# Value products of two attention heads, issued alternately into the two halves of the array's columns

## The reference

```python
def attend(q, k, v):
    s = jnp.einsum('bqhd,bkhd->bhqk', q, k).astype(jnp.float32) * MLA_SCALE
    p = jax.nn.softmax(s, axis=-1).astype(v.dtype)
    return jnp.einsum('bhqk,bkhd->bqhd', p, v)
```

## Time and profile before

| | |
|---|---|
| median of 3 runs | 2709.06 us (2708.07 to 2709.28) |
| profiled execution | 2707.86 us |
| span of its trace | 2706.1 us, 26605 instructions |
| PE busy | 2178.7 us (81%) |
| DVE busy | 1637.9 us (61%) |
| ACT busy | 1122.2 us (41%) |
| POOL busy | 816.2 us (30%) |
| DMA | 940.05 MB, mean 347 GB/s |
| L1664, the edited products | 320 MATMUL records, 46.5 us busy |

### The profile page before, as it was taken

The page is one execution under the profiler, slowest core; times in us unless marked ns, Lnnn a source line. Parts: engine busy times, 40 slices in busy tenths (PEclk is TensorE's granted clock), DMA queues, the critical chain, the costliest instruction groups (busy, mean ns, idle before and its releaser), DMA issues.

```text
span 2706.1 us, 26605 instructions
## 1 busy us (share of the span) xinstructions
PE 2178.7 (81%) x8372; PEld 1023.3 (38%) x8372; DVE 1637.9 (61%) x4029; ACT 1122.2 (41%) x3248; POOL 816.2 (30%) x772
## 2 busy tenths in 40 slices
PE   6998889877788677885777777697889987777776
PEld 4766655432344233441121111176674321221111
DVE  1134476678886756777667775333627666777654
ACT  3233354555773434545343333332423343333333
POOL 0000134434444334344434333100004443343331
PEclk8988999878899889998999999995899999999999
DMA  7883299999999999999999999720018999999997
GB/s 317 316 335 134 72 403 407 409 352 398 413 380 414 421 409 412 417 420 421 421 421 421 421 421 421 312 80 1 17 52 346 425 425 426 426 425 426 426 426 307
DMA packets 133660, 940.05 MB, mean 347 GB/s; under 512 B 14864, under 2 KB 16144, under 8 KB 23312
## 3 DMA queue, kind: packets, MB, share of 16 engines
q0 software_dynamic: 110592, 805.36, 71.9%
q1 hardware_dynamic: 22496, 130.31, 12.2%
q10 hardware_dynamic: 432, 2.70, 0.3%
HBM read 937.26 MB, written 1.05 MB: 347 GB/s over the span
## 4 chain that ended last, share of the span: by engine, by line
DMA 43%; PE 35%; DVE 10%; ACT 8%; issue 3%; POOL 1%; SPq 0%; DVEq 0%; POOLq 0%; ACTq 0%
DMA fast<-uv_dram,idx 26%; DMA mix<-uv_dram,idx 14%; PE bank L1757 11%; PE bank L1716 5%; PE bank L1487 4%; DVE fast L1358 3%; PE bank L1680 2%; DMA qring<-wq_dram 2%; PE bank L1572 2%; PE bank L1451 1%; PE bank L1481 1%; PE bank L1725 1%; ACT diag L933 1%; ACT coef L930 1%; PE bank L1459 1%
## 5 line engine op out<-in xcount | busy, mean ns | idle before, releaser
L1757 PE MATMUL bank<-fast,diag 128*64 128x512 f32 x1956 | 800.4, 657 | 244.3 <-ACT diag L933 242.7
L628 POOL DMA_INDIRECT fast<-uv_dram,idx x489 | 522.4, 1068 | 1422.2 <-PE bank L1757 686.1
L1358 DVE SCALAR_TENSOR_TENSOR fast<-fast,hrow 128x1024 f32<-128x1024 f32 x489 | 598.4, 1225 | 344.9 <-DMA fast<-uv_dram,idx 340.5
L929 ACT ACTIVATE gact<-araw 128x1 f32<-128x1 f32 x768 | 154.4, 201 | 903.5 <-DVE fast L1358 550.5
L1757 PE MATMUL bank<-mix,diag 128*64 128x512 f32 x816 | 382.8, 621 | 102.5 <-ACT diag L933 100.9
L1757 PEld LDWEIGHTS bank<-fast,diag 128*64 128x64 f32 x1956 | 190.7, 144 | 704.7 <-ACT diag L933 458.6
L1358 DVE SCALAR_TENSOR_TENSOR mix<-mix,hrow 128x1024 f32<-128x1024 f32 x204 | 250.3, 1227 | 180.4 <-DMA mix<-uv_dram,idx 175.8
L628 POOL DMA_INDIRECT mix<-uv_dram,idx x204 | 209.5, 1027 | 285.0 <-PE bank L1757 263.8
L933 ACT ACTIVATE diag<-con,coef 128x64 f32<-128x64 f32 x768 | 267.1, 348 | 25.2
L930 ACT ACTIVATE coef<-gact,wts 128x1 f32<-128x1 f32 x768 | 226.2, 295 | 24.9
L1757 PEld LDWEIGHTS bank<-mix,diag 128*64 128x64 f32 x816 | 92.6, 138 | 342.8 <-ACT diag L933 228.3
(11 more groups left out here) (231 smaller groups left out, 2616.6 us busy)
## 6 DMA issues: line engine op xcount, KB each, us to landing
fast<-w_dram SPq DMA_DIRECT2D x72, 1024.0 KB, 8.8
qring<-wq_dram SPq DMA_DIRECT2D x40, 576.0 KB, 8.2
back<-w_dram SPq DMA_DIRECT2D x20, 1024.0 KB, 9.4
fast<-uv_dram,idx POOLq DMA_INDIRECT x489, 17.4
mix<-wq_dram SPq DMA_DIRECT2D x8, 576.0 KB, 5.5
mix<-uv_dram,idx POOLq DMA_INDIRECT x204, 23.9
fast<-uq_dram SPq DMA_DIRECT2D x4, 576.0 KB, 3.5
xT<-x_dram ACTq DMA_DIRECT2D x1, 2048.0 KB, 9.0
```

Of the source, the lines that this page charges most:

```text
L628: g.indirect_dma_start(slot(e, m), None, uv_tabs[e], bass.IndirectOffsetOnAxis(idx[:, Q % 2, n:n + 1], 0)).then_inc(landed[place], 16)
L929: link(a.activation(gact[:, n:n + 1], araw[:, Q % 2, n:n + 1], ACT.Gelu))
L1358: v.scalar_tensor_tensor(out=u, in0=u, scalar=1.0, in1=hrow[:, (2 * i + half) % 3, :], op0=ALU.mult, op1=ALU.mult, accum_out=araw[:, Q % 2 ...
L1757: mm = t_.matmul(acc[half, f * 512:(f + 1) * 512], diag[:, j % DIAGS, :], slot(e, j)[:, D + f * 512:D + (f + 1) * 512], start=(j % SLOTS < ...
```

## The change

The products of the two heads of a pair are issued in one step at time 9, where head 0's were at 7 and head 1's at 9. Within it the loop over key chunks is outside and that over heads inside, so consecutive products go to different halves of the columns. The step waits for both heads' transposed shares; each head's last product still adds one to `pv_mm`. No other generator is edited.

```diff
                 for j in range(8):
-                    for f in range(2):
-                        i, h = 2 * j + f, 2 * (j % 4) + f
-                        yield ATT_AT + ATT_STEP * j + 7 + 2 * f
-                        if f == 0 and j:
-                            t_.wait_ge(attn_out.sem, attn_out.at(p, j))
-                        t_.wait_ge(pt_ready.sem, pt_ready.at(p, i + 1))
-                        n = chunks(p)
-                        for c in range(n):
-                            vv = vr if c < 2 else vc
+                    yield ATT_AT + ATT_STEP * j + 9
+                    if j:
+                        t_.wait_ge(attn_out.sem, attn_out.at(p, j))
+                    t_.wait_ge(pt_ready.sem, pt_ready.at(p, 2 * j + 2))
+                    n = chunks(p)
+                    for c in range(n):
+                        vv = vr if c < 2 else vc
+                        for f in range(2):
+                            h = 2 * (j % 4) + f
                             mm = t_.matmul(bank[3][64 * f:64 * f + 64, 0:P], vv[:, c % 2, h * VD:(h + 1) * VD], pt[:, f, c, :],
                                            start=(c == 0), stop=(c == n - 1))
-                        mm.then_inc(pv_mm.sem, 1)
+                            if c == n - 1:
+                                mm.then_inc(pv_mm.sem, 1)
```

## The result

The changed kernel takes 2718.49 us (median of 6 runs) against 2708.57 for the kernel before (6 runs): ratio 1.0038, 95% interval 1.0024 to 1.0051. It is slower by about 10 us. The time lies in the range (2706 to 2719), near its upper end, but the likeliest case, no measurable change, isn't what happened. It lies outside the forecast's own range of 2708 to 2716; only the part that was added for the rivals takes it in.

What follows compares the result with a forecast made beforehand. Chain of waits: 43% DMA, 35% TensorE, limits differing by stage. Stage 3 -0.04, stage 0 -0.15, stage 1 +3.0 make +2.8 us on 2707.86: 2710.7 (2711.9 beside the median); range 2708 to 2716, widened for rivals to 2706 to 2719.

Steps and rivals of the forecast that it cites:

- the likeliest case, no measurable change: Whole kernel: time within about 0.2% (5.4 us) of the unchanged kernel, chance 0.72.
- The overlap: Value products of both heads, alternating column halves: 1.02 us in place of 2.04, saving 1.02 us per pair at full clock.
- The new stall: TensorE waits before head 1's transpose for ScalarE's copy of head 0's: 0.76 us per pair in stage 3, 0.54 in stage 0.
- Pairs of 4.81 us: Stage 3 (layer 1's attention): a pair takes 4.81 us against 4.98, -0.17 us, five times.
- stage 3 level: Layer 1's attention: pairs -0.85, head -0.95 and tail +1.76 us, in all -0.04 us.
- Stage 0 level if the clock rises at the same time: Layer 0's context tokens: half-clock pairs gain, full-clock pairs about level, tail +1.11 us; in all -0.15 us.
- The clock rival for stage 0: Layer 0's context tokens: holes in each pair delay the full clock until after the last scores; +9 us, 2721 us, chance 0.14.
- Stage 1, +3.0 us: Layer 0's latent tokens, between expert gathers: later ScalarE copies add 3.0 us, first-order sum 3.8, bounds 0 and 7.6.
- the added wait: Stage 1: seven copies of head 0's transposed shares wait about 1.09 us more, delaying GELU, diagonals and exponentials; 3.8 us summed.
- TensorE's gain is hidden, because each pair's diagonals come late anyway: Stage 1: TensorE's saved time was counted as no gain, since its expert products wait for the diagonals.
- a moved clock: Sign of a wrong prediction: stage 0's clock was to rise near 234 us, as before; no size given.
- No overlap: All three stages: the heads' products run one after another, 2.04 us, and the stalls stay; +24 us, 2733 us, chance 0.06.

Runs made afterwards that it cites:

- run 6: Changed kernel with a second buffer for the copied shares and the heads' products one after the other, not alternating: 2702.61 us, 0.9979 of the kernel before.
- Run 4: Changed kernel with a second buffer for the copied transposed shares, used by pairs with odd j: 2694.87 us, 0.9952 of the kernel before.
- run 3: Kernel before with the new order in stages 0 and 3 only, stage 1 keeping the old order: 2709.52 us, 1.0010 of the kernel before.
- run 2: Kernel before with the new order in stage 1 only, stages 0 and 3 keeping the old order: 2714.70 us, 1.0024 of the kernel before.
- run 5: Kernel before; in stage 1 ScalarE's copy of head 0's transposed shares also waits for the previous pair's head 1 products: 2711.44 us, 1.0010.
- run 9: New order in stage 1 only, with head 0's scores of pairs 3 to 7 computed twice there: 2711.74 us, 1.0028 of the kernel before.
- run 12: Changed kernel with head 0's scores of pairs 3 to 7 computed twice in stage 1: 2713.69 us, 1.0028 of the kernel before.
- run 10: Changed kernel, one buffer, with stage 1's value products at step 8 instead of 9: 2707.94 us, 1.0010 of the kernel before.

## Why the prediction was right and wrong

- **The overlap (16 records in 1.02 us between starts).** Right, 1.02 in all alternating kernels. But its saving was counted against 2 x 1.02, two separate groups. Two heads together take 1.51 us without alternation (run 6), so half of the 1.02 us came from standing together. The last row, 16 records in 1.84 us, showed this in part and went unused.
- **The new stall (0.76 us in stage 3, 0.54 in stage 0).** Right: 0.74 and 0.53. Run 4 takes it away and shows that it ate the overlap.
- **Pairs of 4.81 us; stage 3 level.** 4.87 us measured. At an equal moment of the clock's rise stage 3 cost +0.4 us (run 3), forecast -0.04: the pairs are 0.06 us longer than forecast, five times, and the tail 0.2.
- **Stage 0 level if the clock rises at the same time.** It rose seven microseconds earlier after scores(0) in the trace, and the attention gained 2.00 us and the projection, where the clock fell again, lost 1.69. Run 3's trace had it late (34.1 us). The clock rival for stage 0, as written, didn't decide. Its counter-argument, that holes of 0.7 us leave the clock at 1.00, doesn't carry over: here the clock fell in the projection, behind holes of 0.53 to 0.75 us.
- **Stage 1, +3.0 us (bounds 0 and 7.6).** This is the step that failed, by its size: +6.85 us from T(1,0) to T(7,0) in the trace, +9.79 in the piece that holds it, +6.7 timed for stage 1 alone (run 2). The term "the added wait" was near: 2.4 us over six pairs at the full clock (run 5). What was missing is in the sentence "TensorE's gain is hidden, because each pair's diagonals come late anyway". The hidden gain became 2.01 us of idle time where 0.80 was, and behind it the clock fell in three of five places; L1758 then takes 2.6 to 3.3 us for 1.94 just where it, the transposes and V stand in the ring between two ScalarE copies. The price of the clock was put at nothing, and was 6.1 us in this trace, against 1.6 in the kernel before. The clock rival was written for stage 0, on the critical path, and not for the stage where TensorE has slack.
- **The time inside the range.** This is in part luck. The range reached 2719 for the sake of the clock rival in stage 0, and what filled it was mostly stage 1.
- **The clock.** 0.91 in stage 1 against 0.97. The prediction named a moved clock as a sign of being wrong, and it moved. The Trainium skill ("TensorE: Matmul & The Clock Gate", A second HAM failure mode) states that small idle gaps between bursts of matmuls make the clock fall and rise again. The traces agree with it in the mean (idle 2.01 us, 0.91; filled in runs 9 and 12, 1.00 and 0.99), but not place by place: two of five groups behind 2.01 us keep the full clock, in run 9 one behind 3.74 us does, and run 10, with the slot filled elsewhere, has 0.90.
- **No overlap.** Ruled out by every trace.

## What to carry to other kernels

Before grouping work to use the array better, ask what the first half's early end released. Here an interleaved pair finishes both halves together, so a single-buffered operand comes free half a group later; with a second buffer the same edit turned from 10 us slower to 13 us faster. Where an engine has slack, "the gain is hidden" isn't the whole answer: the idle time grows, and the clock of what follows it must be priced too (here 6 us by the traces; the timed runs didn't confirm that filling the gap gives it back).

## What the runs showed of the hardware that I had not expected

- Eight records to one half of the columns followed directly by eight to the other half take 1.51 us to the next start at the full clock. Eight alone take 1.02, alternating 16 take 1.02.
- With the new order and one buffer, 38 records of the output projection behind stage 0 took 10.16 us in four of five traces, and 8.47 in all ten others; TensorE had stood idle for 0.53 us in each pair before them.
- In stage 1, 20 more TensorE records went with a stretch shorter by 5 to 6 us (68.5 and 69.1 us against 74.1 and 74.3), at granted clocks of 1.00 and 0.99 against 0.91.
- At the start of stages 0 and 3 the half clock lasts differently long: the same instructions of stage 0 took 32.7 to 32.9 us in four traces and 30.71 in a fifth, and the new order's of stage 3 46.7 and 49.6. This moves these stages by 2 to 3 us from one execution to the next.
